# The second-last output row of a decoder layer, finished and stored in two halves, the left half ahead of the last row's addition

## What is computed

```python
def _layer_norm(x, g, b):
    mu = jnp.mean(x, axis=-1, keepdims=True)
    var = jnp.mean(jnp.square(x - mu), axis=-1, keepdims=True)
    return (x - mu) * lax.rsqrt(var + NORM_EPS) * g + b

def reference(x, w_in, conv_w, mix_norm_g, w_out, ln1_g, ln1_b, w_gate_up, w_down, ln2_g, ln2_b):
    ...
    x = _layer_norm(DEEPNORM_ALPHA * x + mixed @ w_out[layer], ln1_g[layer], ln1_b[layer])
    gate, up = jnp.split(x @ w_gate_up[layer], 2, axis=-1)
    ffn = (jax.nn.silu(gate) * up) @ w_down[layer]
    x = _layer_norm(DEEPNORM_ALPHA * x + ffn, ln2_g[layer], ln2_b[layer])
    return x
```

## Time and profile before

| | us |
|---|---|
| time, median of 3 runs (lowest, highest) | 1240.17 (1239.91, 1240.55) |
| time of the profiled execution | 1239.94 |
| its span | 1238.2 |
| PE busy | 1217.6 (98%) |
| DVE busy | 950.7 (77%) |
| last matmul ends | 1229.95 after the start of the span |
| last DVE instruction ends | 1235.70 |

### The profile page before, as it was taken

How to read it: one execution, slowest core, us unless ns; L and a number is a source line. 1 busy time by engine, 2 the same in 40 slices (tenths; PEclk the granted TensorE clock), 3 DMA queues, 4 the chain that set the end, 5 groups by cost and what they waited for, 6 DMA issues and landing times.

```text
span 1238.2 us, 17041 instructions
## 1 busy us (share of the span) xinstructions
PE 1217.6 (98%) x6037; PEld 1027.0 (83%) x6037; DVE 950.7 (77%) x1534; ACT 524.7 (42%) x918; POOL 671.0 (54%) x553
## 2 busy tenths in 40 slices
PE   9999999999999999999999999999999999999997
PEld 8988888888788898888788888888888888888885
DVE  4679999999988888347868777676677765565997
ACT  4467322221369889304533333333332334644351
POOL 2330766996978531019978766666666620020744
PEclk9999999999999999999999999999999999999999
DMA  5332122311011130442145454454544458966664
GB/s 205 89 74 51 36 52 60 85 52 27 8 43 44 27 90 6 170 131 95 58 160 186 137 196 142 156 181 138 167 161 136 161 186 314 333 188 198 191 193 164
DMA packets 121980, 157.66 MB, mean 127 GB/s; under 512 B 7316, under 2 KB 81320, under 8 KB 120488
## 3 DMA queue, kind: packets, MB, share of 16 engines
q1 hardware_dynamic: 121896, 156.57, 39.3%
HBM read 109.09 MB, written 40.11 MB: 121 GB/s over the span
## 4 chain that ended last, share of the span: by engine, by line
PE 74%; DVE 21%; ACT 1%; issue 1%; POOL 1%; DMA 0%; SPq 0%; DVEq 0%; ACTq 0%; POOLq 0%
PE banks L751 21%; PE banks L753 21%; PE banks L752 21%; DVE mask L2109 14%; PE banks L1028 2%; PE banks L974 2%; PE banks L1077 2%; PE banks L995 1%; PE banks L996 1%; PE banks L1047 1%; PE banks L1048 1%; DVE scores L2093 1%; DVE tied L2155 1%; DVE pt L2178 1%; DVE scores L2152 1%
## 5 line engine op out<-in xcount | busy, mean ns | idle before, releaser
L2109 DVE TENSOR_SCALAR_CACHE_REDUCE mask<-scores,small 128x384 bf16<-128x384 f32 (+1 forms) x186 | 163.7, 943 | 1.1
L2433 DVE TENSOR_TENSOR step_lo<-step_raw,step_hi 128x1024 fp32r<-128x1024 f32 x77 | 110.5, 1455 | 57.0 <-ACT step_hi L1619 56.2
L1865 POOL TENSOR_TENSOR ring_lo<-sum,ring_hi 128x512 fp32r<-128x512 f32 x88 | 122.4, 1393 | 58.0 <-ACT ring_hi L1555 58.0
L751 PE MATMUL banks<-act_hi,ring_hi 128*128 128x512 f32 x352 | 137.4, 390 | 0.0
L753 PE MATMUL banks<-act_hi,ring_lo 128*128 128x512 f32 x352 | 137.1, 390 | 0.0
L752 PE MATMUL banks<-act_lo,ring_hi 128*128 128x512 f32 x352 | 137.1, 389 | 0.0
L1865 POOL TENSOR_TENSOR ring_lo<-gu_raw,ring_hi 128x512 fp32r<-128x512 f32 x66 | 95.8, 1452 | 66.5 <-ACT ring_hi L1555 66.5
L1619 ACT ACTIVATE step_hi<-step_raw 128x1024 fp32r<-128x1024 f32 x77 | 81.7, 1061 | 111.3 <-DMA step_raw<-in_w_down 55.6
L1555 ACT ACTIVATE ring_hi<-sum 128x512 fp32r<-128x512 f32 x88 | 55.0, 630 | 166.7 <-POOL sum L1876 64.6
L1672 POOL TENSOR_TENSOR w_lo<-w_raw,w_hi 128x384 fp32r<-128x384 f32 (+3 forms) x68 | 73.8, 1105 | 95.5 <-ACT w_hi L1276 94.4
L751 PE MATMUL banks<-step_hi 128*128 128x512 f32 x308 | 120.0, 390 | 0.0
(11 more groups left out here) (272 smaller groups left out, 3178.7 us busy)
## 6 DMA issues: line engine op xcount, KB each, us to landing
gu_raw<-in_w_gate_up SPq DMA_DIRECT2D x44, 512.0 KB, 5.1
step_raw<-h_store SPq DMA_DIRECT2D x77, 256.0 KB, 2.8
wd_raw<-in_w_down SPq DMA_DIRECT2D x11, 1024.0 KB, 4.9
h_store<-hid SPq DMA_DIRECT2D x11, 1024.0 KB, 3.9
step_raw<-wd_store SPq DMA_DIRECT2D x44, 256.0 KB, 3.5
wd_store<-wd_raw SPq DMA_DIRECT2D x11, 768.0 KB, 3.3
h_store<-h_sum SPq DMA_DIRECT2D x11, 768.0 KB, 5.4
step_raw<-in_w_down SPq DMA_DIRECT2D x33, 256.0 KB, 3.2
```

Source lines behind the costliest of these rows:

```text
L751: pe.matmul(dst, a[0], b[0], start=first, stop=False)
L1865: pool.tensor_tensor(ring_lo[:, slot], src, ring_hi[:, slot].bitcast(F32), ALU.subtract).then_inc(ring_low, 1)
L2109: c = dve.tensor_scalar(mask[:, part(b)], scores[:, part(b)], threshold(j), 0.0, ALU.is_ge, ALU.add, accum_out=count[:, j:j + 1])
L2433: dve.tensor_tensor(step_lo[n][:], step_raw[n][:], step_hi[n][:].bitcast(F32), ALU.subtract).then_inc(step_low, 1)
```

## The change

Row 6 is finished in two halves. The left one is written ahead of `add_product` for the last row, the right one stays where the whole was. Each half signals `finished`, and SP stores each half by itself, so that there are four stores of 256 KB for rows 6 and 7 instead of one of 512 KB and two of 256 KB. The final wait counts one store more.

```diff
@@ -735,13 +735,12 @@
             for q, b in enumerate(ROWS3[:6]):
                 sp.wait_ge(normed, NB + q + 1)
                 sp.dma_start(out_rows[b], y2[:, b, :]).then_inc(stored, 16)
-            sp.wait_ge(finished, 1)
-            sp.dma_start(out_rows[ROWS3[6]], y2[:, ROWS3[6], :]).then_inc(stored, 16)
-            for half in range(2):
-                cols_ = slice(half * 512, (half + 1) * 512)
-                sp.wait_ge(finished, 2 + half)
-                sp.dma_start(out_rows[ROWS3[7]][:, cols_], y2[:, ROWS3[7], cols_]).then_inc(stored, 16)
-            sp.wait_ge(stored, 16 * (NB + 1))
+            for q in (6, 7):
+                for half in range(2):
+                    cols_ = slice(half * 512, (half + 1) * 512)
+                    sp.wait_ge(finished, 2 * (q - 6) + half + 1)
+                    sp.dma_start(out_rows[ROWS3[q]][:, cols_], y2[:, ROWS3[q], cols_]).then_inc(stored, 16)
+            sp.wait_ge(stored, 16 * (NB + 2))
@@ -2574,6 +2573,8 @@
             for r in range(4):
                 q = r + 4
+                if q == NB - 1:
+                    finish_row(NB - 2, 0, DM // 2)
                 add_product(6, r, sum_rows(1, 1, r), sum_rows(1, 1, r))
@@ -2581,7 +2582,7 @@
                 if q < NB - 1:
                     apply_gain(q, 0, DM)
                 else:
-                    finish_row(NB - 2, 0, DM)
+                    finish_row(NB - 2, DM // 2, DM // 2)
                     apply_gain(q, 0, DM // 2)
                     apply_gain(q, DM // 2, DM // 2)
```

## The result

| | before | after |
|---|---|---|
| time, median (lowest to highest) of 22 runs each | 1240.28 (1239.87 to 1240.92) | 1241.96 (1241.45 to 1242.67) |
| last matmul ends, in the profiled execution | 1229.95 | 1230.98 |
| from there to the end of the span | 8.21 | 9.82 |

The changed kernel takes 1.0014 times as long, interval [1.0008, 1.0019]: slower, by 1.68 us, which is less than the 0.2% bound of the forecast.

What follows compares the result with a forecast made beforehand. PE is busy 98% of the span, but DVE's chain after the last matmul sets the end. The last addition starts 2.17 later, less 0.54 saved: 1.63 later, so 1240.17 + 1.63 = 1241.80, range 1240.9 to 1242.7.

Steps and rivals of the forecast that it cites:

- The saving behind the variance: Behind row 7's variance, a 1024-column DVE finish becomes one of 512: 1.20 - 0.66 = 0.54 saved.
- the 0.13 that sticks out: Unhindered, the left half would run from 1229.45 to 1230.11, 0.13 beyond the last addition's start at 1229.98.
- The start of the left half: On DVE, the left half can start at 1229.45, 0.10 behind the end of POOL's root of row 6.
- The wait for POOL: Left half stands until POOL's bias of row 5 ends, finishing 0.54 or 0.55 later; last addition 2.17 later.
- What comes after: Behind the addition: row 7's root keeps 0.30 of slack, the landing stays 2.1, the fourth store costs nothing.
- SHARED: Rival: left half and POOL's bias run together at half speed, net +0.25, 1240.4; chance 0.03.
- The gain: Rival: DVE's left half gets in first or unhindered, 0.41 faster, 1239.8, or 1240.2 with later stores; chance 0.06.
- Longer: Rival: POOL's bias of row 5 takes 3.01 instead of 2.35 under contention, net 2.29, 1242.5; chance 0.08.
- The rule that was weighed: VectorE with two SBUF inputs and GpSimd lock a shared port pair for a whole instruction; the other fully blocks.
- Starts first: Part of the skill's port rule: whichever of DVE and POOL starts first gets the port; three trace pairs agree.
- The pair of the earlier trace: POOL started at 73.16, DVE's 512-column instruction at 73.40; DVE took its usual 0.73, POOL ended after it.

Runs made afterwards that it cites:

- e1: The changed kernel with POOL's bias of row 5 cut from 1024 columns to 1, the bias of that row left out: 1239.91.
- e3: The changed kernel with both halves of row 6 put behind the variance of row 7, four stores kept: 1240.74.
- e2: The changed kernel with the left half of row 6 reading its bias from PSUM bank 1, where ACT copied it: 1239.95.
- e4: The changed kernel with a left piece of 256 columns ahead of the addition and a right piece of 768 behind: 1242.13.
- e5: The changed kernel with POOL's bias of row 5 in two instructions of 512 columns: 1241.03.
- e6: The changed kernel with DVE's order kept, but row 6 stored in one piece once both halves are done: 1241.95.
- e10: The changed kernel with two one-column POOL additions between the root of row 6 and the bias of row 5: 1240.50.
- e9: The changed kernel with one one-column POOL addition between the root of row 6 and the bias of row 5: 1242.09.
- e8: The kernel before, with gain and bias for rows 6 and 7 read from PSUM and all of row 6 finished before the last addition: 1239.35.
- e7: The changed kernel with POOL's bias of row 5 waiting until the left half is done: 1240.61.

## Why the prediction was right

It gave 1241.80 (1240.9 to 1242.7) and the measured median is 1241.96. Of the 0.16 between them, 0.11 is that before's median came out at 1240.28 instead of 1240.17. The difference of the medians, 1.68 against 1.63, is known to about 0.7 either way, so its closeness is partly luck; the mechanism rests on the tails and durations.

- **The saving behind the variance**, 0.54: e1 measures it together with the 0.13 that sticks out, 0.39 against 0.41. In e3 the same two halves cost 0.14 where 2 x 0.66 - 1.20 = 0.12 was due.
- **The start of the left half**, 0.10 behind the root's end: in after the root ends at 1228.87 + 1.52 = 1230.39 and the half starts at 1230.50.
- **The wait for POOL**: ended 0.55 behind POOL, forecast 0.54 or 0.55. The addition is 2.16 later against the last matmul (2.20 instead of 0.04), forecast 2.17. e1 and e2 show that this is the conflict over a second SBUF input, and e4 and e5 that it lasts as long as POOL's instruction.
- **What comes after**: the rest of the chain shifted as a whole, the root of row 7 was not late, and the stores cost nothing (e6). Here one piece was wrong without effect: the root took 1.01, not 1.54, so it ended at 1236.10, 0.83 ahead of the finish of row 7 and not 0.30.
- **The rivals**: SHARED fell to e4. The gain exists (e1, e2), but not in this order of events. "Longer" took L1961's 3.01 in the earlier trace rows for a possible price of contention; POOL took 2.35 in after and 2.79 in e10, where it was the one to stand. So the 3.01 fits POOL's own standing, as I had read it, and not a price of contention.
- **The rule that was weighed**: the runs bear out the exclusive lock for a whole instruction (the Trainium skill, SBUF — State Buffer, "SBUF: two separate sides"). "Starts first" holds only roughly in profiled starts: DVE lost with a lead of 0.02 (e9) and won with none (e3, at 690.67) and with 0.04 (the pair at 751.8). Within these hundredths the profiled starts do not say who gets the port, and what does is not shown. The pair of the earlier trace rows, where DVE won although POOL's start lay 0.24 earlier, comes out the same way in the traces of all twelve kernels; no run was aimed at it, and it stays open.

## What to carry to other kernels

Before moving a DVE instruction into a gap, look at what POOL does in that gap: if both read SBUF, the DVE one takes two tensors from there and POOL's is under way first, the gap isn't free, and the price is what is left of POOL's instruction, however short DVE's piece is (2.76 for 512 columns, 2.50 for 256). A constant operand copied to a free PSUM bank takes the DVE instruction out of the conflict (e2, e8); a shorter POOL instruction limits it (e5); a later start of POOL's moved it here to the next DVE instruction of the kind, and the store behind POOL's with it (e7, e10). A standing instruction looks like a slow one in the profile, so compare its duration with that of the same shape elsewhere before believing that it is work.

## What the runs showed beyond that

POOL's root on one column took 1.52 wherever it started beside a DVE gain with two SBUF inputs (and all profiles but e8's in this place). In e8, with the gain read from PSUM, the same instruction takes 0.55. Beside a 512-column one with two SBUF inputs it takes 1.01 (after), though not beside one with its gain in PSUM (0.55 again, e8's root of row 7). Wherever it takes 1.01 or 1.52 it ends 0.40 or 0.41 behind DVE's instruction: 1229.35 against 1228.95 in before, in after 1236.10 against 1234.94 + 0.75 = 1235.69. So even this small instruction stood for the port in before, about 1 us each time, and the root of row 6 could be ready 1 us earlier, as it is in e8. In the prediction I had taken 1.52 for the price of the power itself.
